# Second layer's experts: gathered key and value rows replaced by one-hot tables over all experts

## The reference

```python
def one_chunk(xt):                       # xt: 128 tokens, normed; two chunks
    q = (xt @ w_q).reshape(BLOCK, PEER_HEADS, PEER_QDIM)       # 8 heads, 256 wide
    s1 = einsum('chd,nd->chn', q[..., :half], keys1)           # 128 scores
    s2 = einsum('chd,nd->chn', q[..., half:], keys2)           # 128 scores
    t1, i1 = lax.top_k(s1, 16);  t2, i2 = lax.top_k(s2, 16)
    cand = t1[..., :, None] + t2[..., None, :]                 # 256 candidates
    cidx = i1[..., :, None] * 128 + i2[..., None, :]
    ts, sel = lax.top_k(cand, 16)
    idx = take_along_axis(cidx, sel)                           # 16 of 16384 experts
    g = softmax(ts)
    act = gelu(einsum('chkd,cd->chk', u[idx], xt))             # key rows
    return einsum('chk,chkd->cd', g * act, v[idx])             # value rows
```

## Time and profile before

| | |
|---|---|
| median of 3 runs | 1437.83 us (1436.86 to 1438.47) |
| profiled execution | span 1437.5 us from first to last instruction; its own time is not listed apart, the median stands 0.3 us above this span |
| TensorE busy | 1289.3 us, 90% of the span |
| VectorE busy | 848.4 us, 59% |
| ScalarE busy | 422.1 us, 29% |
| GpSimd busy | 292.7 us, 20% |
| bytes moved by DMA | 367.98 MB, of them 269.50 MB in the gathers' queue |

### The profile page before, as it was taken

How to read it: one execution, slowest core, us unless ns; L and a number is a source line. 1 busy time by engine, 2 the same in 40 slices (tenths; PEclk the granted TensorE clock), 3 DMA queues, 4 the chain that set the end, 5 groups by cost and what they waited for, 6 DMA issues and landing times.

```text
span 1437.5 us, 19206 instructions
## 1 busy us (share of the span) xinstructions
PE 1289.3 (90%) x7268; PEld 833.1 (58%) x7268; DVE 848.4 (59%) x2097; ACT 422.1 (29%) x974; POOL 292.7 (20%) x269
## 2 busy tenths in 40 slices
PE   7999998999999999999999989999877777777776
PEld 4446788986579878887888544444333332333322
DVE  7527866546563247232115867777777777777654
ACT  1215223121351136453003243333322322223212
POOL 0000000000000100000003344456543444444420
PEclk9999999999999999999999999999999999999999
DMA  9444100343324344432457999999999999999994
GB/s 308 158 151 133 33 3 3 118 146 117 118 89 151 110 136 148 127 106 88 146 209 297 421 421 403 421 421 421 421 421 421 421 421 420 422 421 420 422 422 202
DMA packets 68972, 367.98 MB, mean 256 GB/s; under 512 B 9295, under 2 KB 12751, under 8 KB 35793
## 3 DMA queue, kind: packets, MB, share of 16 engines
q0 software_dynamic: 37152, 269.50, 45.3%
q1 hardware_dynamic: 31586, 96.99, 20.4%
q10 hardware_dynamic: 144, 0.26, 0.0%
HBM read 365.67 MB, written 1.06 MB: 255 GB/s over the span
## 4 chain that ended last, share of the span: by engine, by line
PE 55%; DMA 24%; DVE 7%; ACT 2%; issue 1%; DVEq 0%; ACTq 0%
PE bank L1845 16%; PE bank L2491 11%; DMA arena<-peer_in,arena 7%; DMA row<-peer_in,arena 7%; DMA cst<-peer_in,arena 7%; PE bank L2437 3%; PE bank L1383 3%; DMA res<-peer_in,arena 2%; PE bank L1463 2%; PE bank L1440 2%; PE bank L805 2%; PE bank L614 1%; PE bank L604 1%; PE bank L1515 1%; PE bank L2425 1%
## 5 line engine op out<-in xcount | busy, mean ns | idle before, releaser
L2491 PE MATMUL bank<-arena 128*128 128x512 f32 x584 | 276.7, 614 | 65.1 <-ACT arena L2595 65.1
L2491 PEld LDWEIGHTS bank<-arena 128*128 128x128 f32 x584 | 109.1, 194 | 218.2 <-issue 217.9
L1845 PE MATMUL bank<-arena,ring 128*128 128x256 f32 (+2 forms) x1104 | 232.3, 371 | 2.2 <-DVE arena L2266 1.4
L1845 PEld LDWEIGHTS bank<-arena,ring 128*128 128x128 f32 x1104 | 198.8, 190 | 32.0 <-DVE arena L2266 1.8
L2732 DVE CUSTOM_DVE_ANT_0 arena<-arena 128x1024 f32<-128x1024 f32 x146 | 176.8, 1222 | 54.6 <-DMA arena<-peer_in,arena 54.4
L2777 POOL DMA_INDIRECT arena<-peer_in,arena x146 | 167.3, 1146 | 183.5 <-PE bank L2491 162.0
L2595 ACT ACTIVATE arena<-cst,arena 128x128 f32<-128x128 f32 x256 | 88.9, 394 | 133.8 <-DVE arena L2681 132.5
L2587 ACT ACTIVATE arena<-arena 128x2 f32<-128x2 f32 x129 | 38.0, 295 | 261.6 <-DVE arena L2732 261.5
L2491 PE MATMUL bank<-ring,arena 128*128 128x512 f32 x160 | 76.7, 623 | 21.7 <-ACT arena L2595 21.6
L2777 POOL DMA_INDIRECT row<-peer_in,arena x18 | 19.3, 1072 | 312.5 <-DVE arena L2669 276.3
L2491 PE MATMUL bank<-cst,arena 128*128 128x512 f32 x140 | 68.7, 624 | 13.6 <-ACT arena L2595 13.5
(11 more groups left out here) (400 smaller groups left out, 1982.1 us busy)
## 6 DMA issues: line engine op xcount, KB each, us to landing
ring<-stream_in SPq DMA_DIRECT2D x155, 512.0 KB, 3.6
ring<-stream_in SPq DMA_DIRECT2D x8, 384.0 KB, 6.5
arena<-stream_in SPq DMA_DIRECT2D x6, 512.0 KB, 7.2
arena<-peer_in,arena POOLq DMA_INDIRECT x146, 33.4
row<-rows_in SPq DMA_DIRECT2D x4, 512.0 KB, 18.7
cst<-cst_in SPq DMA_DIRECT2D x1, 1868.0 KB, 18.5
row<-rows_in POOLq DMA_DIRECT2D x2, 512.0 KB, 6.3
cst<-rg_w_in SPq DMA_DIRECT2D x1, 1024.0 KB, 7.9
```

The source lines that it names most:

```text
L1845: mm = nc.tensor.matmul(bank[:, first:first + width], slot[:, at + k * cols:at + (k + 1) * cols], src[:, k, :], start=k == 0, stop=k == kt ...
L2491: mm = nc.tensor.matmul(core.banks[2 * t + b][:, :], diag[i % ND], value_half(i, b), start=False, stop=last)
```

## The change

- The tensor `peer` and the gathers are gone. The key table `u` and the value table `v` join the stream of weights: 128 slots `pu` (slot j holds the key rows of the 128 experts whose second digit is j) and 128 slots `pv`.
- `mix` is done for all 256 tokens at once, then all 16 query tiles, and the ring is cut to 4 places (`LATE_RING`); the other half of it holds new buffers.
- `meet_keys(j)`: 8 products of 128 x 256 give the dots of all 256 tokens with the 128 experts of slot j. Two j make a pair (64 pairs) and fill one bank. ScalarE puts gelu of it in the table `G` (`open_pair`).
- The picks stay as two digits and a share per pick. They are transposed, and for each token a one-hot matrix of the first digits times the share, and one of the second digits, are made (`weigh_ones` on VectorE, `make_ones` on GpSimd, four tokens to a group, 64 groups); a product of the two (`spread`) gives the token's 128 x 128 table of shares. VectorE multiplies it into `G` (`weave`). This is done during pairs 40 to 63: what of the table is not yet open then receives the shares first (`copy_rest`) and the gelu is set aside (`spare`) and multiplied in by GpSimd (`meet`).
- `meet_values(j, t)`: with `G` as stationary operand, the 128 value slots are multiplied in full: 2 token halves x 2 column halves of 128 x 512 for each j.

The rest of the kernel keeps its order; VectorE's routing is one unit after another, with no dots between.

```diff
-EARLY = 7
+LATE_RING = 4
...
+    out += [((name, j), D) for name in ("pu", "pv") for j in range(NK)]
...
-            panel("mix", m, tiles(Y, T)[:, :, 0:P], KT, P, bank=bank).then_inc(*full(("mix", 0, m)))
+            panel("mix", m, tiles(Y, T), KT, T).then_inc(*full(("mix", m)))
...
-                        mm = nc.tensor.matmul(core.banks[2 * t + b][:, :], diag[i % ND], value_half(i, b),
-                                              start=False, stop=last)
...
+        def meet_keys(j):
+            key = ("u", j // 2)
+            bank = core.banks[core.bank_at[key][0]] if j % 2 else claim(pe, key, 4 + j // 2 % 2)
+            slot = core.weights(pe, ("pu", j))
+            for k in range(KT):
+                mm = nc.tensor.matmul(bank[:, j % 2 * T:(j % 2 + 1) * T], slot[:, k * P:(k + 1) * P], normal[:, k, :], start=k == 0, stop=k == KT - 1)
...
+        def spread(q):
+            bank = claim(pe, key, 6 + q % 2)
+            pe.wait_ge(ones_weighed.handle, q + 1)
+            pe.wait_ge(ones_made.handle, q + 1)
+            for i in range(QUAD):
+                mm = nc.tensor.matmul(bank[:, i * NK:(i + 1) * NK], ONES[q % HELD][:, i, 0, :], ONES[q % HELD][:, i, 1, :], start=True, stop=True)
...
+        def meet_values(j, t):
+            slot = core.weights(pe, ("pv", j))
+            for b in range(2):
+                mm = nc.tensor.matmul(core.banks[2 * t + b][:, :], G[:, j, t * P:(t + 1) * P], half(slot, b), start=False, stop=j == NK - 1)
...
+        for p in range(PAIRS):
+            if p == WEAVE:
+                for t in range(TT):
+                    turn_picks(t)
+            for j in (2 * p, 2 * p + 1):
+                meet_keys(j)
+            for q in groups(p):
+                spread(q)
+        pe.wait_ge(woven.handle, GROUPS // 2)
+        for j in range(LAST):
+            meet_values(j, 0)
...
+        def open_pair(p):
+            bank = filled(act, ("u", p))
+            before = done_by(p - 1) * QUAD
...
+                ins = nc.scalar.activation(tiles(spare[n % 2], T)[:, :, 0:before], halves[:, :, 0:before], ACT.Gelu_apprx_tanh)
...
+                nc.scalar.activation(G[:, 2 * p:2 * p + 2, before:], halves[:, :, before:], ACT.Gelu_apprx_tanh).then_inc(*opened.up())
...
+                nc.scalar.activation(G[:, first:, tokens_of(q)], by_key[:, first:, :], ACT.Copy).then_inc(*rest_copied.up())
...
+        def weigh_ones(q):
+            for i in range(QUAD):
+                n = q * QUAD + i
+                ins = nc.vector.tensor_scalar(ONES[q % HELD][:, i, 0, :], cst("iota"), index_t[:, n, 0:1], weight_t[:, n:n + 1],
+                                              ALU.is_equal, ALU.mult)
...
+        def weave(q):
+            dve.wait_ge(opened.handle, min(p + 1, opened.count))
+            if rest_copied.count > q:
+                dve.wait_ge(rest_copied.handle, q + 1)
+            bank = filled(dve, key)
+            nc.vector.tensor_tensor(at, at, by_key[:, 0:2 * (p + 1), :], ALU.mult).then_inc(*woven.up())
+            dve.wait_ge(woven.handle, q + 1)
+            dve.sem_inc(*free(key))
...
+        for q in range(GROUPS):
+            if q + 1 < GROUPS:
+                weigh_ones(q + 1)
+            weave(q)
...
-            pool.indirect_dma_start(out=places[seat[i]], out_offset=None, in_=g.names["peer"],
...
+                ins = nc.gpsimd.tensor_scalar(ONES[q % HELD][:, i, 1, :], cst("iota"), index_t[:, n, 1:2], None, ALU.is_equal)
...
+            nc.gpsimd.tensor_tensor(at, at, tiles(spare[n % 2], T)[:, :, 0:before * QUAD], ALU.mult).then_inc(*met.up())
```

More of the change, by code:

```diff
@@ L206, in pack_weights @@
     out = []
-    for key, width in weight_slots() + first_queries():
+    for key, width in weight_slots():
         if key == "lora":
@@ L2452, in turn @@
[L2452 to L2462 removed]
+        core.rotation, core.next_bank = [4, 5, 6, 7], 0
@@ new lines, in query @@
+        def query(h):
+            key = ("wq", h)
+            bank = claim(pe, key)
+            for i in range(2):
+                slot = core.weights(pe, ("wq", 2 * h + i))
+                for k in range(KT):
+                    if h == 0 and i == 0:
+                        pe.wait_ge(g.gained.handle, k + 1)
+                    mm = nc.tensor.matmul(bank[:, i * T:(i + 1) * T], slot[:, k * P:(k + 1) * P], n2[:, k, :], start=k == 0, stop=k == KT - 1)
+                if i:
+                    mm.then_inc(*full(key))
+                    core.used_by(("wq", 2 * h + i), key)
+                else:
+                    mm.then_inc(*core.used_now(("wq", 2 * h + i)))
@@ new lines, in scores, with sum_squares @@
+        def scores(h):
+            key = ("score", h)
+            copied(pe, ("wq", h))
+            bank = claim(pe, key)
+            for t in range(TT):
+                for i in range(2):
+                    mm = nc.tensor.matmul(bank[:, (2 * t + i) * NK:(2 * t + i + 1) * NK], QT_[h % 2][:, i * T + t * P:i * T + (t + 1) * P],
+                                          keys[:, i * NK:(i + 1) * NK], start=True, stop=True)
+            mm.then_inc(*full(key))
+        def sum_squares():
+            bank = claim(pe, "ss_d")
+            for k in range(KT):
+                pe.wait_ge(squared.handle, k + 1)
+                mm = nc.tensor.matmul(bank[:, 0:T], cst("ones"), squares[:, k, :], start=k == 0, stop=k == KT - 1)
+            mm.then_inc(*full("ss_d"))
@@ new lines, in _ @@
+        for m in range(KT):
+            square_in(m)
+        query(0)
+        bank = filled(act, "ss_d")
+        nc.scalar.activation(rstd_all, bank[:, 0:T], ACT.Sqrt, bias=g.eps[:, 0:1], scale=1.0 / D).then_inc(*free("ss_d"))
+        query(1)
+        scores(0)
+        for h in range(2, HP):
+            query(h)
+            scores(h - 1)
+        scores(HP - 1)
+        for p in range(PAIRS):
+            if p == WEAVE - 1:
+                for t in range(TT):
+                    exps(t)
+            if p == WEAVE:
+                for t in range(TT):
+                    lay(t)
+            open_pair(p)
+            for q in groups(p):
+                copy_rest(q)
@@ L2781, in _, with lk @@
[L2781 to L2789 removed]
+        def lk(ins):
+            link(pool, "pool", ins)
```

724 lines of the change are left out of this document (313 added, 411 removed).

## The result

The changed kernel takes **1816.8 us** (median of 3 runs, 1815.4 to 1818.6) against 1437.8: ratio 1.263, with its 95% interval 1.260 to 1.267. The forecast was 1808 with a range of 1784 to 1842. The profiled execution spans 1814.9 us, 8.9 more than the 1806 of the sum.

A forecast was written before the change was run, and what follows sets the result against it. Gathers at 421 GB/s bound the old last stage; TensorE's products would bound the new one. 737.5 + 1041 + 0.7 + 22 + 5.1 = 1806 us of span, plus 0.3 and 1.5 for small waits: 1808, range 1784 to 1842.

The forecast's parts named there:

- the sum: Whole kernel's span: 737.5 us up to the mix, 1041 of TensorE work, 0.7, 22 of idle and 5.1 of tail, 1806.
- the second rival: Pairs 40 to 63: VectorE's one-hot rows wait for GpSimd operations, 18 us more, 1826 us; chance 0.20.
- Bound before: Last stage of the old kernel: bound by 256 gathers of 1 MB, 637 us at 421 GB/s.
- The price of one product: TensorE, float32: two records a product; 0.434 us for 128 x 256, 0.858 for 128 x 512, 0.225 for 128 x 128.
- What I cost at nothing: Stream, routing, gelu, normed tokens, VectorE's add and gain before a query: all taken as hidden behind TensorE's work, 0 us.
- The idle in the pairs: Pairs 40 to 63: TensorE waits for the third group's bank and one-hot rows, 1.4 us, 16 times, 22 us.
- Hand-offs hidden: Pairs 40 to 63: the third spread's chain is shorter than thought, so 22 us vanish, 1785 us; chance 0.12.
- VectorE and GpSimd hold each other up: Pairs 40 to 63: one-hot rows wait for GpSimd, sometimes also a `meet`, 1.1 x 16 = 18 us, 1826; chance 0.20.
- the doubled weaving: Weaving in pairs 40 to 63, reading its bank in steps of 128 elements: doubled time would add 10 us.
- GpSimd bounds the pairs: Pairs 40 to 63: at 1.1 us an operation GpSimd takes 12.9 us a pair, 62 us more, 1868; chance 0.06.
- the other side: `meet_keys` and `meet_values`: no slower than before; with one record a product the time would be 1286 us; chance 0.02.

## Why the prediction was right

The forecast of 1808 missed by 8.8 us, 0.5%. The number alone doesn't tell it from the second rival, whose 1826 is 9.2 us away on the other side; the runs do.

- **Bound before.** Confirmed by the halved gathers, which freed 5%.
- **The price of one product** made the result. Two records a product, 0.434 and 0.858 us: measured (276.45 - 0.16) / 640 = 0.432 and (439.63 - 0.16) / 512 = 0.858. Keys came to 442 against 444.2, values to 439.6 against 439.5. The 0.434 had kept the last record's overlap that it meant to take off: (55.52 - 0.16) / 128 is 0.4325. That it is a price of TensorE's time and not a mean with waits in it is shown by half the keys (214 of 221 us) and by bfloat16 (a quarter).
- **What I cost at nothing.** The stream held (two places cost 61 us, four none; at half the work per slot, four cost 2.9). Routing ended at 913 us, against 916. GpSimd's element operation I took at 0.3 us; it is 0.605, between the bounds from the earlier trace rows. The guess was off by two, and its length cost nothing only because GpSimd has 10.7 us a pair for 10.7 rows, 6.5 us, and a `meet` of 0.73. In the bfloat16 kernel the same error would have decided.
- **The idle in the pairs** is the step that was mis-sized: "The idle is 1.4 us, 16 times: 22 us". By the timeline above, its terms were: opening 0.86 (0.8 said), copying the rest 0.49 with its hand-off (0.3), weaving 0.67 (0.5 to 0.68), the wait of VectorE for itself 0.25 and four rows 1.32 (0.9 for the rows, 0.3 for all hand-offs), start of the spread 0.10. The loss is 1.96 or 2.28 a pair; with one stretch of lower clock it is 34.5 by the run without third groups, 12.5 above the 22. Keys, spreads and transposes that were shorter than said gave 3.8 back, which leaves 8.7. The four rows were priced from a pair of one-pointer operations. These take two pointers and stood behind a wait; they last 1.12 us with no GpSimd operation beside them, and 0.2 more beside GpSimd's rows. Part of the small miss is luck: the terms as I wrote them add up to 2.8 to 3.1 us, not to 3.2, so 2 to 6 of the 22 us stood on nothing.
- **Rivals.** *Hand-offs hidden* (1785) did not happen, but it is what the rows made ahead (1786.8) and the two groups (1779.2) make of the kernel, so its place was right. *VectorE and GpSimd hold each other up* (1826) does happen, but at 2.9 us, not 18: beside GpSimd's one-hot rows the four rows of VectorE lose 0.2 us a stop, and in the changed kernel no `meet` falls on them. That its 18 lies near the real surplus of 12.5 is chance. With the doubled weaving its own terms give 1836, so the range's end of 1842 had 6 us that no term explains. *GpSimd bounds the pairs* and *the other side* stayed out, the latter by the doubled records alone.

The idle takes only a few values. The twelve of 1.74 us are alike because the copy of the rest shrinks (0.32 to 0.18 us from the second stop to the fifteenth) as the weaving grows (0.51 to 0.67), and the rows take up the remainder (1.33 to 1.30), every second of them starting 0.04 us behind a start of GpSimd's. The four of 2.06 have 0.44 us instead of 0.09 between the copy's end and the weaving. The same four stops have it with GpSimd silent and without the wait for oneself; why is open.

## What to carry to other kernels

Before replacing gathers of picked rows by dense products over all rows, count the records of one product of that type in the trace, and their length in a dense stretch: here 128 times the wanted key dots and the dense values take 882 us of TensorE in float32, where the gathers took 637 us of DMA, while in bfloat16 a product takes a quarter and the plan wins by 13% over the float32 kernel with gathers. Ask also what the thing removed was hiding: with half the gathers' bytes gone the old kernel gained only 5%. And in a hand-ordered engine queue, put work that others wait for ahead of work that must wait, and a wait for one's own result behind everything that doesn't need it.

## What the hardware showed that I had not expected

- **An engine's wait for its own operation costs more than its gap.** On VectorE, taking it from between a weaving and a one-hot row brought the row forward from 0.82 to 0.50 us after the weaving's start, 5.4 us over 16 stops. TensorE's idle fell by 7.2.
- **VectorE's one-hot rows wait for GpSimd.** Four take 1.12 us with GpSimd idle, 1.17 to 1.33 beside its one-hot rows, and up to 1.89 beside a `meet`, which a row waits out. A busy sum over the stage (378 against 363 ns a row) doesn't show it: taking work off one engine let the rest of its work move onto the chain.
- **A short stop can cost clock.** In the run with GpSimd silent, TensorE had been dense but for stops of 1.5 to 2.4 us in two of three pairs. Its timeline has five blocks of 32 key records longer than 7.07 us, of which one is

```profile
1225.16 1.95 PE L2452 MATMUL bank<-ring 128*128 128x128 f32 x16
1228.99 1.73 PE L2452 MATMUL bank<-ring 128*128 128x128 f32 x8 [1.89 <-issue]
1230.51 8.18 PE L2429 MATMUL bank<-res,ring 128*128 128x256 f32 x32
```

and its windows show the clock:

```profile
1226.00:1230.00 4.00, 2.12 (x16) 1.95 (x16) 2.56 (x8) 0.53 (x3) 0.64 (x1) 0.92 0.44 133
1230.00:1234.00 4.00, 4.00 (x16) 3.40 (x14) 2.44 (x8) 0.26 (x1) 0.00 (x0) 0.66 0.00 0
1234.00:1240.00 6.00, 6.00 (x36) 5.46 (x35) 0.04 (x1) 0.91 (x3) 0.17 (x1) 1.00 0.40 101
```

The granted clock falls towards the lower of its two levels (1.2 GHz) behind the stop, and is back at the upper one (2.4 GHz) in the third window. The five blocks are 5.3 us longer than 7.07 each, and the spreads ahead of them 3.1 us longer than 1.13 each. All five stand behind stops of 1.89 to 2.38 us that are the second in two neighbouring pairs; stops of 1.92 to 2.33 that came first of the two had no slow block behind them. The changed kernel has one such block, 1.7 us with its spread, behind a stop of 2.06, the run with half the keys two, behind 2.06 and 2.02, and the run without the self-wait, whose stops are 1.74 at most, none. Why three other stops of 2.06 in the changed kernel cost nothing is open.
- **GpSimd's elementwise row of 128 elements takes 0.605 us**, twice VectorE's 0.287. No run has it at a second size, so how much of it is fixed isn't known. For the `meet` the trace of the changed kernel has 23 sizes:

```profile
L2781 POOL TENSOR_TENSOR arena<-arena,ring 128x496 f32<-128x496 f32 x1 | 1.2, 1228 | 5.8 <-ACT ring L2542 5.8
L2781 POOL TENSOR_TENSOR arena<-arena,ring 128x128 f32<-128x128 f32 x1 | 0.5, 452 | 0.0
L2781 POOL TENSOR_TENSOR arena<-arena,ring 128x24 f32<-128x24 f32 x1 | 0.2, 231 | 0.0
```

From the smallest and the largest, an estimate is 0.18 us fixed and 2.1 ns an element, so there most of the time goes with the elements from some 90 on.
